# A two-block kernel with S5 and gated linear attention on one core: S5 tables without zeros, their products on half the array, and another order of the small products on TensorE

## The reference

```
p = u @ ev_w_in            # a_in, a_z, b_val, b_gate, b_z, 1024 columns each
# S5, 64 groups g of 16 channels, 64 complex states each:
s_t = Lbar s_(t-1) + Bbar u_t ;  y_t = Re(C s_t) + D u_t
ya = gelu(y) ; ya = ya * sigmoid(ya @ w_glu + b_glu) * silu(a_z)
yb = conv31(b_val * sigmoid(b_gate)) -> layernorm -> silu -> @ w_pw ; yb = yb * silu(b_z)
x = x + rmsnorm(concat(ya, yb) @ ev_w_out)
```

## Time and profile before

| | |
|---|---|
| median of 3 runs (lowest, highest) | 1731.13 us (1730.51, 1733.36) |
| the profiled execution | 1731.83 us |
| its span, first to last instruction | 1730.1 us |
| TensorE busy | 1661.8 us, 96% of the span |
| VectorE, ScalarE, GpSimd busy | 930.0, 661.9, 203.2 us |
| granted TensorE clock, mean | 0.987 of full speed |

### The profile page before, as it was taken

How to read it: one execution, slowest core, us unless ns; L and a number is a source line. 1 busy time by engine, 2 the same in 40 slices (tenths; PEclk the granted TensorE clock), 3 DMA queues, 4 the chain that set the end, 5 groups by cost and what they waited for, 6 DMA issues and landing times.

```text
span 1730.1 us, 20069 instructions
## 1 busy us (share of the span) xinstructions
PE 1661.8 (96%) x7876; PEld 1355.4 (78%) x7876; DVE 930.0 (54%) x1293; ACT 661.9 (38%) x914; POOL 203.2 (12%) x234
## 2 busy tenths in 40 slices
PE   6999989999999999998999998999989999999997
PEld 5888878878888888887988887767867777787775
DVE  3267263544235423555999997753545444454445
ACT  5333232133221223334454543655335344352442
POOL 4990000000000000004123220112000000000000
PEclk9999999999999999999999999999999999999999
DMA  8464532242333332216869984867213123131211
GB/s 252 120 176 128 142 97 97 74 146 85 110 98 98 98 97 98 98 61 245 190 160 205 193 187 135 184 144 184 86 49 115 56 74 97 48 110 56 77 49 61
DMA packets 151228, 206.75 MB, mean 120 GB/s; under 512 B 51964, under 2 KB 74988, under 8 KB 150124
## 3 DMA queue, kind: packets, MB, share of 16 engines
q1 hardware_dynamic: 131915, 173.62, 32.6%
q0 software_dynamic: 17568, 29.89, 10.7%
q10 hardware_dynamic: 1664, 2.13, 0.4%
HBM read 190.94 MB, written 14.68 MB: 119 GB/s over the span
## 4 chain that ended last, share of the span: by engine, by line
PE 91%; ACT 3%; DVE 2%; DMA 1%; issue 1%; SPq 0%; ACTq 0%; DVEq 0%
PE PS L2040 78%; PE PS L2018 2%; PE PS L2269 1%; PE PS L2321 1%; PE PS L2339 1%; PE PS L2194 1%; PE PS L2330 1%; PE PS L2161 1%; DMA T<-d_tm 1%; ACT XN L910 1%; DMA WL<-in_conv_w_pw_dram 1%; PE PS L2349 0%; PE PS L2113 0%; PE PS L2310 0%; PE PS L2243 0%
## 5 line engine op out<-in xcount | busy, mean ns | idle before, releaser
L2040 PE MATMUL PS<-HH,WH 128*128 128x512 f32 x1216 | 477.9, 393 | 10.3 <-issue 5.4
L2040 PE MATMUL PS<-HL,WH 128*128 128x512 f32 x1216 | 475.2, 391 | 0.0
L2040 PE MATMUL PS<-HH,WL 128*128 128x512 f32 x1216 | 474.9, 391 | 0.0
L903 ACT ACTIVATE WH<-WR 128x1024 fp32r<-128x1024 f32 x200 | 211.8, 1061 | 657.9 <-PE PS L2040 644.6
L1331 DVE TENSOR_TENSOR WL<-WR,WH 128x1024 fp32r<-128x1024 f32 x144 | 186.9, 1306 | 424.5 <-ACT WH L903 424.4
L2040 PEld LDWEIGHTS PS<-HH,WH 128*128 128x128 f32 x1216 | 229.6, 189 | 60.0 <-issue 10.4
L2040 PEld LDWEIGHTS PS<-HL,WH 128*128 128x128 f32 x1216 | 229.6, 189 | 48.3 <-issue 1.0
L2040 PEld LDWEIGHTS PS<-HH,WL 128*128 128x128 f32 x1216 | 229.5, 189 | 48.2
L2040 PE MATMUL PS<-WH,HH 128*128 128x512 f32 x384 | 154.7, 403 | 9.7 <-DVE WL L1331 4.2
L1713 DVE SCALAR_TENSOR_TENSOR TMP<-CP,PRM,TMP 128x512 f32<-128x512 f32 x232 | 154.9, 746 | 0.0
L2040 PE MATMUL PS<-WH,HL 128*128 128x512 f32 x384 | 152.6, 397 | 0.0
(11 more groups left out here) (327 smaller groups left out, 1951.8 us busy)
## 6 DMA issues: line engine op xcount, KB each, us to landing
WR<-in_w_in_dram SPq DMA_DIRECT2D x96, 512.0 KB, 3.7
WR<-in_od_w_in_dram SPq DMA_DIRECT2D x32, 512.0 KB, 3.9
WR<-in_ev_w_in_dram SPq DMA_DIRECT2D x24, 512.0 KB, 4.5
WL<-in_ev_w_in_dram POOLq DMA_DIRECT2D x24, 512.0 KB, 7.8
WR<-in_ev_w_in_dram SPq DMA_DIRECT2D x32, 256.0 KB, 3.2
WR<-in_ev_w_out_dram SPq DMA_DIRECT2D x16, 512.0 KB, 4.2
WR<-in_od_w_in_dram SPq DMA_DIRECT2D x32, 256.0 KB, 3.3
WR<-in_od_w_out_dram SPq DMA_DIRECT2D x16, 512.0 KB, 3.8
```

What stands on the lines that cost most here:

```text
L903: act.activation(WH[:, n % RING, :, :], WR[:, n % RING, :, :], ACT.Copy).then_inc(w_hi, 1)
L2040: mm = pe.matmul(out_banks[m], st, mv, start=(kt == 0 and i == 0), stop=(kt == 2 * per - 1 and i == 2))
```

## The change

The order on TensorE becomes: a_u, sgu_t, a_z, w_t.0, g0.0, w_t.1, g0.1, sgu.0, sgu.1, k.0, k.1, b_p; and later b_z2.0, s5_y.0, s5_y.1, y_t.0, b_z2.1, y_t.1, glu; in ev_a the first six means stand behind the whole of ev_a.0. `w_t` are 32 transposes of 128x128. `k` runs bank by bank, 16 products of one half of the array after each other. `s5_y` has for each pair and each of its two groups three products of 64 rows, 128 chunks and 64 columns, in runs of three on a half of the array. `d_g` and `d_tm` hold no zeros and aren't filled with any; they are read in whole before a_z2's weights. `free_bank` waits for one bank, not four, where the job two places before has four evacuations by one engine; all sections but w_out and ev_b, the turns, sgu, k, s5_y and ev_a use it. VectorE does sgu_out before the lags, and 24 and 26 taps around y_t.0 instead of 58 before it; in the rest of its program the order is the same.

The diff, cut to its core (the moved `sgu_out` is unchanged; GpSimd's mask for sgu_t moves ahead of the powers of Lbar; counts of semaphores follow):

```diff
@@ -82,15 +82,16 @@
+_add("sgu_t", side=1, a=2)
...
-for _i in range(4):
-    _add(f"w_t.{_i}", side=1, a=2, d=2)
-_add("sgu_t", side=1, a=2)
-_section("g0", a=4)
+_add("w_t.0", side=1, a=2, d=2)
+_add("g0.0", 4, 0, 4)
+_add("w_t.1", side=1, a=2, d=2)
+_add("g0.1", 4, 0, 4)
+for _i in range(2):
+    _add(f"sgu.{_i}", side=1, d=4)
...
-for _i in range(2):
-    _add(f"sgu.{_i}", side=1, d=4)
@@ -117,11 +118,12 @@
-_section("b_z2", a=4)
+_add("b_z2.0", 4, 0, 4)
...
-for _i in range(2):
-    _add(f"y_t.{_i}", side=4, d=4)
+_add("y_t.0", side=4, d=4)
+_add("b_z2.1", 4, 0, 4)
+_add("y_t.1", side=4, d=4)
@@ -287,7 +291,7 @@
-WTS = put("WTS", "R3", [2, PAIRS, 64])
+WTS = put("WTS", "R3", [2, PAIRS // 2, P])
@@ -308,8 +312,8 @@
-VT = [put("VT_0", "R3", [2, PAIRS // 2, P]), put("VT_1", "HL", [2, PAIRS // 2, P])]
-T6 = [put("T6_0", "R5", [PAIRS // 2, P], skip=8192), put("T6_1", "HH", [PAIRS // 2, P])]
+VT = put("VT", "R3", [2, 2, PAIRS // 2, 64])
+T6 = put("T6", "R5", [PAIRS, 64], skip=8192)
@@ -329,7 +333,7 @@
-YT = put("YT", "R3", [T4, D])
+YT = [put("YT_0", "R6", [T4, NC]), put("YT_1", "R3", [T4, NC])]
@@ -369,8 +373,8 @@
-d_g = nc.dram_tensor("d_g", [P, 2, PAIRS, P], F32, kind="Internal").ap()
-d_tm = nc.dram_tensor("d_tm", [P, PAIRS, P], F32, kind="Internal").ap()
+d_g = nc.dram_tensor("d_g", [P, 2, PAIRS, 64], F32, kind="Internal").ap()
+d_tm = nc.dram_tensor("d_tm", [P, PAIRS, 64], F32, kind="Internal").ap()
@@ -528,7 +526,7 @@
     sp.wait_ge(zeroed, 1)
-    for m in (d_wt[:, 0], d_wt[:, 1], d_g[:, 0], d_g[:, 1], d_tm):
+    for m in (d_wt[:, 0], d_wt[:, 1]):
@@ -537,15 +535,19 @@
     sp.wait_ge(pool_g, 1)
-    halves_out(d_g[:, 0], lambda h: GRE[h, :, 1:5, :].rearrange("p r t q -> p r (t q)"), s5_out)
-    halves_out(d_g[:, 1], lambda h: GNI[h, :, 1:5, :].rearrange("p r t q -> p r (t q)"), s5_out)
-    sp.wait_ge(banks_act, act_after("w_t.3"))
-    sp.wait_ge(banks_dve, dve_after("w_t.3"))
+    for ri, lags in enumerate((GRE, GNI)):
+        sp.dma_start(d_g[:, ri], lags[:, :, 1:5, :].rearrange("p r t q -> p r (t q)")).then_inc(s5_out, 16)
+    sp.wait_ge(banks_act, act_after("w_t.1"))
+    sp.wait_ge(banks_dve, dve_after("w_t.1"))
...
-        halves_out(d_wt[:, ri], lambda h: WTS[h, ri, :, :], s5_out)
+        for b in range(2):
+            for g in range(2):
+                half = slice(64 * g, 64 * g + 64)
+                sp.dma_start(d_wt[half, ri, :, half].rearrange("p (r b) n -> p b r n", b=2)[:, b],
+                             WTS[64 * b:64 * b + 64, ri, :, half]).then_inc(s5_out, 16)
...
-    halves_out(d_tm, lambda h: TM[h, :, :], s5_out)
+    sp.dma_start(d_tm, TM[:, :, :]).then_inc(s5_out, 16)
@@ -579,22 +581,12 @@
     sp.wait_ge(side_done, side_after("s5_z.3"))
...
-    vt_in_half(0)
-    t6_in_half(0)
+    for i in range(2):
+        sp.dma_start(VT[:, i, :, :, :], d_g[:, :, 16 * i:16 * i + 16, :]).then_inc(vt_in, 16)
+    sp.dma_start(T6[:, :, :].rearrange("p r n -> p (r n)"), d_tm.rearrange("p r n -> p (r n)")).then_inc(t6_in, 16)
...
-    sp.wait_ge(weights_used, used_after("b_z2.1"))
-    vt_in_half(1)
-    t6_in_half(1)
@@ -1009,27 +1000,30 @@
     act.activation(STAT[:, 2, :], BNA[:, :, 1], ACT.Sqrt, bias=EPS[:, 1:2]).then_inc(v_std, 1)
-    split()
-    act.wait_ge(zeros_out, 16 * 10)
-    via_tmp("a_z.0", ACT.Silu)
-    split()
-    via_tmp("a_z.1", ACT.Silu)
+    split(2)
...
-    for i in range(4):
-        act.wait_ge(side_done, side_after(f"w_t.{i}"))
-        for ri in range(2):
-            act.activation(WTS[0:64, ri, 8 * i:8 * i + 8, :],
-                           bank(f"w_t.{i}", 2 * ri)[0:64, :].rearrange("p (r n) -> p r n", r=8),
-                           ACT.Copy).then_inc(banks_act, 1)
+    act.wait_ge(side_done, side_after("sgu_t"))
...
-        if not m:
-            act.wait_ge(side_done, side_after("sgu_t"))
...
+    split(2)
+    act.wait_ge(zeros_out, 16 * 4)
+    via_tmp("a_z.0", ACT.Silu)
+    split()
+    via_tmp("a_z.1", ACT.Silu)
+    def wts_out(i):
+        act.wait_ge(side_done, side_after(f"w_t.{i}"))
+        for m in range(2):
+            act.activation(WTS[:, 0, 8 * i + 4 * m:8 * i + 4 * m + 4, :].rearrange("p r n -> p (r n)"),
+                           bank(f"w_t.{i}", m), ACT.Copy).then_inc(banks_act, 1)
+    wts_out(0)
...
+    wts_out(1)
@@ -1144,22 +1138,24 @@
     evac("b_z2.0", [BZ[:, m, :] for m in range(4)], ACT.Silu)
-    split()
-    for m in range(4):
-        act.wait_ge(side_done, side_after("s5_y.0", m + 1))
-        act.activation(BZ[:, 4 + m, :], bank("b_z2.1", m), ACT.Silu).then_inc(banks_act, 1)
+    act.wait_ge(fixed, 2)
...
-            act.wait_ge(side_done, side_after(f"s5_y.{i}", m + 1) if i else side_after("s5_y.0"))
-            kt = 4 * i + m
-            dst = YT[:, :, kt * P:(kt + 1) * P].rearrange("c t (x q) -> c x t q", q=S5_GROUP)
-            act.activation(dst, bank(f"s5_y.{i}", m).rearrange("p (x t q) -> p x t q", x=8, t=T4),
+            act.wait_ge(side_done, side_after(f"s5_y.{i}", m - m % 2 + 2))
+            dst = YT[i][:, :, :].rearrange("c t (r g q) -> c r g t q", g=2, q=S5_GROUP)[:, 4 * m - 4 * (m % 2):4 * m - 4 * (m % 2) + 8, m % 2]
+            act.activation(dst, bank(f"s5_y.{i}", m).rearrange("p (r t q) -> p r t q", r=8, t=T4),
...
-    for i in range(2):
+    def y_out(i):
...
+    y_out(0)
+    split()
+    evac("b_z2.1", [BZ[:, 4 + m, :] for m in range(4)], ACT.Silu)
+    y_out(1)
@@ -1430,13 +1426,34 @@
     dve.wait_ge(consts, 4)
-    for i in range(4):
+    def wts_out(i):
...
-        for ri in range(2):
-            dve.tensor_copy(WTS[64:P, ri, 8 * i:8 * i + 8, :],
-                            bank(f"w_t.{i}", 2 * ri + 1)[64:P, :].rearrange("p (r n) -> p r n", r=8)).then_inc(banks_dve, 1)
-    split()
-    split()
+        for m in range(2):
+            dve.tensor_copy(WTS[:, 1, 8 * i + 4 * m:8 * i + 4 * m + 4, :].rearrange("p r n -> p (r n)"),
+                            bank(f"w_t.{i}", 2 + m)).then_inc(banks_dve, 1)
+    wts_out(0)
+    split()
+    wts_out(1)
+    split()
+    dve.wait_ge(bs_in, 16)
+    dve.wait_ge(tmp_free, 8)
...
+    sgu_out(0)
+    sgu_out(1)
@@ -1734,10 +1736,12 @@
         pass
-    convolve(58)
+    convolve(24)
...
+        if i:
+            convolve(26)
@@ -1992,6 +1996,19 @@
             pe.wait_ge(h_lo if prev[5][0] == "h" else y_lo, prev[5][1])
+    def free_bank(name, m):
+        i = NAMES.index(name)
+        if i < 2:
+            return
+        a, d = JOBS[i - 2][3:5]
+        if (a, d) == (4, 0):
+            pe.wait_ge(banks_act, _sum(3, i - 2) + m + 1)
+        elif (a, d) == (0, 4):
+            pe.wait_ge(banks_dve, _sum(4, i - 2) + m + 1)
+        elif m == 0:
+            free(name)
@@ -2057,14 +2074,16 @@
             job = f"{name}.{u}"
-            free(job)
+            if by_tile:
+                free(job)
...
-                 rows, tok, per=per, by_tile=by_tile and u == 1)
+                 rows, tok, per=per, by_tile=by_tile and u == 1,
+                 bank_ready=None if by_tile else (lambda m: free_bank(job, m)))
...
-        free(job)
...
+            free_bank(job, m)
@@ -2101,32 +2120,46 @@
     section("a_u", H, ready(h_lo, 0))
-    section("a_z", H, ready(h_lo, 0))
-    pe.wait_ge(pool_w, 1)
-    for i in range(4):
-        free(f"w_t.{i}")
-        for r in range(8):
-            for m in range(4):
-                ri, g = m // 2, m % 2
-                half = slice(64 * g, 64 * g + 64)
-                mm = pe.matmul(bank(f"w_t.{i}", m)[half, r * 64:(r + 1) * 64],
-                               WST[half, ri, 8 * i + r, :, :].rearrange("p j q -> p (j q)"), ident[half, half],
-                               start=True, stop=True)
-        mm.then_inc(side_done, 1)
...
-    section("g0", H, ready(h_lo, 0))
+    section("a_z", H, ready(h_lo, 0))
+    def w_t(i):
+        free(f"w_t.{i}")
+        for m in range(4):
+            for r in range(4):
+                k = 8 * i + 4 * (m % 2) + r
+                mm = pe.transpose(bank(f"w_t.{i}", m)[:, r * P:(r + 1) * P],
+                                  WST[:, m // 2, 2 * k:2 * k + 2, :, :].rearrange("p r j q -> p (r j q)"), ident[:, :])
+        mm.then_inc(side_done, 1)
+    pe.wait_ge(pool_w, 1)
+    w_t(0)
+    section("g0", H, ready(h_lo, 0), units=(0,))
+    w_t(1)
+    section("g0", H, ready(h_lo, 0), units=(1,))
+    pe.wait_ge(v_done, 4)
+    pe.wait_ge(banks_act, act_after("sgu_t"))
+    for i in range(2):
+        for m in range(4):
+            free_bank(f"sgu.{i}", m)
+            g = 4 * i + m
+            for t in range(TT):
+                mm = pe.matmul(bank(f"sgu.{i}", m)[:, t * P:(t + 1) * P], V[:, t, g * P:(g + 1) * P], SGWT[:, g, :],
+                               start=True, stop=True)
+        mm.then_inc(side_done, 1)
...
-        free(f"k.{i}")
-        for r in range(8):
-            for m in range(4):
+        for m in range(4):
+            free_bank(f"k.{i}", m)
+            for r in range(8):
@@ -2134,18 +2167,6 @@
```

(90 more changed lines are left out.)

34 lines of the change are left out of this document (12 added, 22 removed).

## The result

The changed kernel takes 1717.84 us (median of 4 runs, 1716.59 to 1720.52), beside 1732.1 us (1730.51 to 1733.36, 4 runs) for the kernel before on the same chip: a ratio of 0.992, 95% interval 0.9903 to 0.9937. Timed once more on another occasion it took 1718.49 us against 1733.09, 0.9913 (0.99 to 0.9927). It is faster by 14.3 and 14.6 us, 0.8 to 0.9%. The forecast was 1711, the range 1700 to 1727. The profiled execution took 1718.19 us for a span of 1716.5. Between the spans of the two traces the gain is 13.6 us, where the sum said 20.1.

The account below looks back on a forecast made before the run. TensorE, busy 96% of the span, was taken as the bound; 0.7 + 8.0 + 4.3 + 0 + 2.8 + 4.3 = 20.1 us off the profiled 1731.83 gives 1711.7, with the median 0.7 lower: 1711 us, range 1700 to 1727.

Parts of the forecast that it names:

- rival 4: New waits grow: d_wt's writes hold b_p.0's weights, taps hold moments, idle lowers the clock; +5 to +8, 1717; chance 0.16.
- a_u, sgu_t, a_z: Start of the kernel: bank-wise wait saves 1.3 us at a_u, 0.6 new wait at a_z.0; net gain 0.7 us.
- w_t: 32 full transposes replace 128 small products, with 0.55 us of wait estimated at g0.0; gain 8.0 us.
- sgu before k: Stretch before b_p: idle and low clock go, sgu 7.7, k 11.4, delay 1; gain 4.3 us (bounds -1 and +7).
- the delay of 1 us: At b_p.0: late d_wt writes delay its loads and splits ahead of g0.1's evacuation and sgu_out; 0 to 2.6 us.
- S5 outputs: s5_y's products: streaming halved, weight loads bind each half side by side, 21.9 us as before; gain 0.
- Rival 1: Halves of the array take turns: k 15.3, s5_y 43.8 us; +25.8, 1737, slower; chance 0.17, half of it partial overlap.
- rival 2: Weight loads don't bind, 64 rows take half the time: s5_y 11.5 us; -10.4, 1701; chance 0.17.
- Around them: Around s5_y: the 2.4 us wait for d_tm goes, glu waits 2.2 instead of 2.6; gain 2.8 us.
- ev_a: Moved moments remove the 4.1 us YO wait and 2.7 slow stretch, less 2.5 new wait; gain 4.3 (1.5 to 6.8).
- d_wt writes: SyncE's writes after w_t.1, some 16 us later than before, feared to hold up b_p.0's weights.
- Rival 3: k's halves stay side by side, s5_y as forecast: gain 6.3 for 4.3, 1709; shares chance 0.50 with the forecast.

Follow-up runs that it names:

- run by pairs: Changed kernel with k alone altered: banks filled two at a time, products of the array's two halves in turn; 1712.92 us (one run).
- run with a third left out: Changed kernel with s5_y leaving out two VT products of every pair's second group, so one half has 64 records, not 192; 1730.88 us.
- second trace: The changed kernel traced once more, unaltered, beside the kernel with all four edits; 1718.49 us, five runs.
- four edits: Changed kernel plus k by pairs of banks, early table loads, 32 and 32 taps, pw.1's first split before ev_a.1's copies; 1704.9 us.

## Why the prediction was right, and where it was off

The sign and the range were right, and so was the main mechanism, what bounds products on half of the array. The sum was 6.5 us too favourable between the spans, and the prediction's own price for new waits and low clock (rival 4) came nearer than its forecast. By its own steps:

- **a_u, sgu_t, a_z.** The wait for `V` went (1.3 us); a_z.0 waits 0.9 where 0.6 was estimated. 0.4 us instead of 0.7.
- **w_t.** w_t.0 is 16 transposes in 1.9 us, w_t.1 the same, g0.0 waits 0.3 (0.55 estimated). But g0.1 waits 1.5 us, and this term had nothing for it. The step that failed is "half of them now stand between a_z.1 and g0.0": I looked at the place of w_t.0 and not at that of w_t.1. There ScalarE has a split, a change of table and the copy of bank 0 ahead of g0.1. 6.2 us instead of 8.0.
- **sgu before k.** No gap, no low clock at b_p.0, as predicted. sgu took 7.1 us for 7.7 and the delay of 1 us did not come, but k took 13.8 us between bounds of 7.7 and 15.3; the middle, 11.4, was a guess with no mechanism behind it. 3.4 us instead of 4.3, so most of its error was covered by two others. The wait of 2.0 us behind `KS` ahead of sgu, which the prediction's list of waits left out, lay in this stretch and went with it. The run by pairs shows what decides, the length of a run on one half: with the halves in turn k has its old pace of 0.029 again and takes 8.8 us, with VectorE's banks in it.
- **S5 outputs.** 21.85 us for a forecast of 21.9, by the mechanism named: loads bind, each half for itself, both side by side. Rival 1 would have needed 43.8 and rival 2 11.5; the run with long runs shows that rival 1 is real where 24 products of one half follow each other, and the run with a third left out shows rival 2's premise false. TensorE: Matmul & The Clock Gate, of the Trainium skill (LDWEIGHTS), had the load by columns alone, 107 ns for 128; the 188 ns of 64 rows beside the 192 of 128 agree on the columns, and the pace of 0.112 us comes near its figure.
- **Around them.** The wait for `d_tm` is gone. glu.0 waits 2.4 us where 2.2 was forecast, with the table load in it that the text had named. 2.2 us instead of 2.8.
- **ev_a.** The largest miss, 0.8 instead of 4.3 (2.7 in the second trace). The waits came out in sum: 4.1 behind `YO` went, 1.7 came at the means (2.5 forecast), 0.5 more for pw's weights and 0.3 for ev_a's, 1.6 us less in all, which is what the text had. What failed is the clock in "the wait of 4.1 goes, and so does the slow stretch behind it", 2.7 us: slow stretches of 1.6 and 1.7 us came at glu and at pw.1 instead, the one at glu behind a wait of 2.4 that the text had forecast and given no price in clock. In the second trace only the one at glu came. The run with the old order shows besides that the means had nothing to win by their new place: its waits add up to the same. "The wait of 1.4 for the pw weights stays" was wrong by 0.5.
- **The end.** 1.0 us is lost in the last 96 matmuls (23.06 for 22.06), in a part that the change does not touch and not in the second trace: chance, as are the 1.4 us won at the start. The two nearly cancel.

Rival 4 named the right kind of trouble, new waits that grow and an idle time that turns the clock down, and its 1717 is what came, though not by its sum alone: about half of the shortfall is in terms that it doesn't name (w_t's second half, k, the last stretch). Of its three mechanisms two had a part: VectorE's taps, and the clock. The d_wt writes held nothing, but by little: sgu_out starts 3.9 us after sgu, as soon as sgu.0 is done, and VectorE had ended the splits of b_p.0's weights only 0.2 us before. In the runs by pairs and with four edits the chain goes through these splits. Rival 3 (k side by side, 1709) is what the kernel by pairs makes true: its gain over the changed kernel in that stretch is 5.0 us.

## What to carry to other kernels

Products on half of the array run side by side only if the two halves are issued close together: alternate after one to three products, not after a bank. Then price them by the weight columns of one half, not by the number of matmuls; here that made s5_y exactly as long as before. Where a reordering removes a wait, find the engine whose last piece of work bounds the end of that stretch (here VectorE's taps) before the wait is booked as a gain: the old order had as much waiting in it, and what made the difference was moving taps into idle time and one split ahead of four copies. Look at each new neighbour of a small job for a change of ScalarE's table between a split and a copy; a one-element activation placed earlier took 1.4 us off each of two waits.

## What the runs showed of the hardware that was not expected

- The granted clock fell to 0.50 with TensorE's row showing no gap at all, in two runs, one trace of each: in s5_y with 24 products of a half in a row, and with one half at a third of its matmuls. In the changed kernel, with both halves loaded alike and in turn, it stayed at 1.00 for all of s5_y. But it also stayed at 1.00 through the 13.8 us of k, with 16 products of a half in a row, so one half working alone is not enough to explain the fall; its cause stays open.
- Waits of about 2 us are followed by low clock in some executions and not in others: behind 2.4 us at glu in seven of nine traces with that wait (45.4 us for 192 matmuls; 43.82 in the run with k by pairs and in the one with less on one half), at pw.1 behind 1.9 and 2.0 us, but not behind 1.8, 1.6 or 1.5, and not behind 2.6 us at g0.0 in the run that waits for four banks (22.08 us for 96). Each such stretch costs 1.6 to 1.7 us. So two single traces of the same kernel can differ by that much without any other difference, and small gains in this kernel are better read stage by stage than from one total.
